# Two passes for the values of joint attention, a last projection split by tokens, and a residual spilled without its norm

## What is computed

```python
x = x + gmlp_mixer(rms_norm(x, a_norm_g), ...)
k, v = shared_kv(x, kv_norm_g, w_kv)
x = x + chunk_attention_mixer(rms_norm(x, b_norm_g), k, v, b_w_qz, b_rel_bias, b_w_out)  # 16 heads of 64
x = rms_norm(x, final_norm_g)            # end of the first block
h = rms_norm_2(x, norm_g)
y_a = hgrn2_branch(h ...)                # 8 heads of 128
y_b = mla_branch(h ...)                  # 8 heads of 128
merged = gates[0] * (y_a @ w_proj_a) + gates[1] * (y_b @ w_proj_b)
x = x + merged @ w_out                   # the last projection
return rms_norm_2(x, final_norm_g_2)
```

## Time and profile before

| | |
|---|---|
| median of three runs | 1359.68 us |
| profiled execution, its own time | 1360.59 us |
| its span, first to last instruction | 1358.8 us |
| mean granted TensorE clock | 0.992 |
| TensorE busy | 1306.7 us (96%) |
| VectorE, ScalarE, GpSimd busy | 719.0, 646.5, 493.8 us |
| DMA read, written | 124.97 MB, 10.49 MB |

### The profile page before, as it was taken

The page is one execution under the profiler, slowest core; times in us unless marked ns, Lnnn a source line. Parts: engine busy times, 40 slices in busy tenths (PEclk is TensorE's granted clock), DMA queues, the critical chain, the costliest instruction groups (busy, mean ns, idle before and its releaser), DMA issues.

```text
span 1358.8 us, 16181 instructions
## 1 busy us (share of the span) xinstructions
PE 1306.7 (96%) x6346; PEld 1084.1 (80%) x6346; DVE 719.0 (53%) x1256; ACT 646.5 (48%) x957; POOL 493.8 (36%) x206
## 2 busy tenths in 40 slices
PE   6999999999999999999998899999999999999985
PEld 4787888888888888888876788888887888888864
DVE  6464646552236465554766376766626546642325
ACT  4344444542334556464435466656546545542211
POOL 2454344434444323322334433333333333234430
PEclk9999999999999999999999999999999999999998
DMA  5542232334232322322224322222223222234421
GB/s 222 187 139 87 92 99 82 93 101 156 94 108 93 92 78 80 104 62 72 68 82 147 109 63 62 72 78 68 78 93 96 73 80 87 88 103 153 131 62 62
DMA packets 42155, 132.31 MB, mean 97 GB/s; under 512 B 6944, under 2 KB 9696, under 8 KB 41440
## 3 DMA queue, kind: packets, MB, share of 16 engines
q1 hardware_dynamic: 36704, 116.41, 27.2%
q10 hardware_dynamic: 5376, 14.87, 3.1%
HBM read 124.97 MB, written 10.49 MB: 100 GB/s over the span
## 4 chain that ended last, share of the span: by engine, by line
PE 78%; DVE 11%; ACT 6%; issue 2%; DMA 1%; POOL 1%; ACTq 0%; DVEq 0%; SPq 0%
PE banks L462 24%; PE banks L464 24%; PE banks L463 24%; DVE hd L1805 1%; PE banks L624 1%; PE banks L613 1%; DVE naccb L1705 1%; ACT L1232 1%; POOL wlo L452 1%; DVE hb L1802 1%; ACT L1233 1%; PE banks L856 1%; DVE acc L1478 1%; PE banks L735 1%; DMA x_kept<-x 1%
## 5 line engine op out<-in xcount | busy, mean ns | idle before, releaser
L452 POOL TENSOR_TENSOR wlo<-raw,whi 128x1024 fp32r<-128x1024 f32 (+2 forms) x202 | 493.6, 2446 | 829.8 <-ACT whi L973 829.8
L462 PE MATMUL banks<-hhi,whi 128*128 128x512 f32 x752 | 304.7, 405 | 4.5 <-POOL wlo L452 3.3
L973 ACT ACTIVATE whi<-raw 128x1024 fp32r<-128x1024 f32 (+2 forms) x202 | 210.2, 1041 | 201.8 <-PE banks L464 149.4
L464 PE MATMUL banks<-hlo,whi 128*128 128x512 f32 x752 | 294.3, 391 | 0.0
L463 PE MATMUL banks<-hhi,wlo 128*128 128x512 f32 x752 | 294.1, 391 | 0.0
L462 PE MATMUL banks<-yhi,whi 128*128 128x512 f32 x448 | 176.5, 394 | 0.0
L464 PE MATMUL banks<-ylo,whi 128*128 128x512 f32 x448 | 174.6, 390 | 0.0
L463 PE MATMUL banks<-yhi,wlo 128*128 128x512 f32 x448 | 174.4, 389 | 0.0
L462 PEld LDWEIGHTS banks<-hhi,whi 128*128 128x128 f32 x752 | 142.0, 189 | 33.2 <-issue 5.6
L464 PEld LDWEIGHTS banks<-hlo,whi 128*128 128x128 f32 x752 | 141.6, 188 | 30.6
L463 PEld LDWEIGHTS banks<-hhi,wlo 128*128 128x128 f32 x752 | 142.0, 189 | 26.8 <-issue 1.9
(11 more groups left out here) (359 smaller groups left out, 2116.1 us busy)
## 6 DMA issues: line engine op xcount, KB each, us to landing
raw<-w SPq DMA_DIRECT2D x194, 512.0 KB, 3.5
rel_tab<-relx ACTq DMA_DIRECT2D x1, 4096.0 KB, 21.4
tab<-rel_tab SPq DMA_DIRECT2D x16, 224.0 KB, 3.5
x<-xt SPq DMA_DIRECT2D x4, 512.0 KB, 6.5
x<-xt ACTq DMA_DIRECT2D x1, 2048.0 KB, 8.1
x_kept<-x ACTq DMA_DIRECT2D x1, 2048.0 KB, 7.3
parts_kept<-mcg SPq DMA_DIRECT2D x8, 256.0 KB, 4.4
mgt<-parts_kept SPq DMA_DIRECT2D x8, 256.0 KB, 3.9
```

The costliest lines, as they stand in the source:

```text
L452: nc.gpsimd.tensor_tensor(wlo[:, n % 4, 0:width], raw[:, n % 2, 0:width], f32(whi[:, n % 4, 0:width]), ALU.subtract).then_inc(lo_done, 1)
L462: nc.tensor.matmul(dst, a[0], b[0], start=first, stop=False)
L464: return nc.tensor.matmul(dst, a[0], b[1], start=False, stop=last)
L973: nc.scalar.activation(whi[:, n % 4, 0:width], raw[:, n % 2, 0:width], ACT.Copy).then_inc(hi_done, 1)
```

## The change

**Attention.** For each pair there are now two value tiles: in the one for head q, the 64 columns of side q hold the high half of that head's values and the other 64 the low half. A matmul with `phi` and one with `plo` then give the high terms in the rows of side q and the low terms in the other rows. ScalarE copies the low rows to `ao` (`lower_terms`), VectorE adds the two (`sum`), and the multiplication by `az` becomes a step of its own (`gated`), after this pair's maxima. Head 0 writes bank 0 instead of 2, head 1 bank 2 instead of 7 (at the last pair 7 and 2), so t=3 waits for head 1 only. `at_values` writes halves of 64 columns.

**Residual.** The spill is of `x` without the norm, issued on ScalarE's queue after the last slab `w2`. The diagonal, the wide matmul and the eight multiplications for it move to the loop of the `pb` slabs (`normed`).

**Last projection.** Tokens are done in two halves of 256, in the order `W3_ORDER` (g is the half, m the slab). The first three half slabs run k 0 to 6 first. Slabs 4 to 7 are kept in `yhi`, `ylo`, and their cuts wait for no buffer. The squares of the last tile are summed by TensorE itself; mean, reciprocal and root are on 128x2 (`factors`), and spread as at the border. Half 0 is normed and stored while half 1 is computed. `norm` is gone.

```diff
+W3B = (2, 3, 0, 1)
+W3_ORDER = [(0, 0), (0, 1), (1, 0), (0, 2), (0, 3), (1, 1), (0, 4), (0, 5), (1, 2), (0, 6), (0, 7),
+            (1, 3), (1, 4), (1, 5), (1, 6), (1, 7)]
+TOK_AT = 11
+OUT0 = [range(0), range(0, 3), range(3, 6), range(6, 8)]
+KEPT = AT["w3", KT // 2]
+HALF = [slice(S // 2 * g, S // 2 * (g + 1)) for g in range(2)]
...
+AO = [(0, 2)] * (PAIRS - 1) + [(7, 2)]
...
+        def av_at(q, half, t, side):
+            return av[q][:, 4 * half:4 * half + 4, t, BD * side:BD * (side + 1)]
...
+        def parts(n):
+            if n < KEPT:
+                return whi[:, n % 4, :], wlo[:, n % 4, :]
+            tiles = slice(2 * (n - KEPT), 2 * (n - KEPT) + 2)
+            return [u[:, tiles, :].rearrange("p k n -> p (k n)") for u in (yhi, ylo)]
...
-                        pe.wait_ge(auV.sem, auV.at("y0", i - 1))
+                        pe.wait_ge(auV.sem, auV.at("sum1", i - 1))
...
             def at_attended(i):
+                pe.wait_ge(auV.sem, auV.at("plo1", i))
                 for q in (1, 0):
-                    pe.wait_ge(auV.sem, auV.at("plo1", i))
                     for k in range(TT):
...
+                        for p in (phi, plo):
+                            last = nc.tensor.matmul(bank[AO[i][q]][:, k * P:S], av[q][:, i, k, :],
+                                                    p[:, q, AK[q][k]:AK[q][k] + KW[k]], start=k == 0 and p is phi,
+                                                    stop=k == TT - 1 and p is plo)
                     last.then_inc(auP.did(f"o{q}"), 1)
 
             at_values(0)
             for i in range(PAIRS):
+                if i >= 2:
+                    pe.wait_ge(auV.sem, auV.at("sum0", i - 2))
...
+            pe.wait_ge(auV.sem, auV.at("sum0", PAIRS - 2))
...
-                        for g in range(2):
-                            wide = nc.tensor.matmul(bank[3 - g], ones, diag[:, g, :], start=True, stop=True)
-                        wide.then_inc(n2P.did("wide"), 1)
+                        nc.tensor.matmul(bank[3], ones, diag[:, 0, :], start=True, stop=True).then_inc(n2P.did("wide"), 1)
...
+                if m == 1:
+                    pe.wait_ge(x3V.sem, x3V.at("diag"))
+                    nc.tensor.matmul(bank[5], ones, nfull[:, 1, :], start=True, stop=True).then_inc(x3P.did("wide"), 1)
...
-            pe.wait_ge(mgV.sem, mgV.all())
-            for m in range(KT):
-                if m >= 4:
-                    pe.wait_ge(w3V.sem, w3V.at(f"x{m - 4}"))
-                slab("w3", m, bank[m % 4], (mgh, mgl))
-            norm(n3, w3V.sem, w3V.all())
+            def out_slab(at, ks=range(KT)):
+                g, m = W3_ORDER[at]
+                n = AT["w3", m]
+                pe.wait_ge(lo_done, n + 1)
+                hi, lo = parts(n)
+                for k in ks:
+                    if at == 0:
+                        pe.wait_ge(mgV.sem, mgV.at("lo", k))
+                    cols = slice(k * P, (k + 1) * P)
+                    last = mm3(bank[W3B[at % 4]][:, HALF[0]], (hi[:, cols], lo[:, cols]),
+                               (mgh[:, k, HALF[g]], mgl[:, k, HALF[g]]), k == 0, k == KT - 1)
...
+            def out_tokens(g):
+                pe.wait_ge(w3V.sem, w3V.at(f"acc{g}{KT - 2}"))
+                pe.wait_ge(w3A.sem, w3A.at(f"sq{g}{KT - 1}"))
+                for b in range(2):
+                    blk = slice(S // 2 * g + P * b, S // 2 * g + P * (b + 1))
+                    to = bank[7][:, 2 * g + b:2 * g + b + 1]
+                    nc.tensor.matmul(to, nacc[:, blk], ones[:, 0:1], start=True, stop=False)
+                    tok = nc.tensor.matmul(to, nsq[:, (KT - 1) % 2, blk], ones[:, 0:1], start=False, stop=True)
+                tok.then_inc(w3P.did(f"tok{g}"), 1)
+
+            def out_wide(g):
+                pe.wait_ge(w3V.sem, w3V.at(f"diag{g}"))
+                nc.tensor.matmul(bank[6 - g][:, HALF[0]], ones, nr[:, 0, HALF[g]], start=True,
+                                 stop=True).then_inc(w3P.did(f"wide{g}"), 1)
+
+            pe.wait_ge(mgA.sem, mgA.all())
+            for at in range(2):
+                out_slab(at, done_keys)
+            pe.wait_ge(mgV.sem, mgV.at("b", KT - 2))
+            out_slab(2, done_keys)
+            for at in range(3):
+                out_slab(at, last_key)
+            for at in range(3, 2 * KT):
+                if at >= 4:
+                    g, m = W3_ORDER[at - 4]
+                    pe.wait_ge(w3V.sem, w3V.at(f"x{g}{m}"))
+                out_slab(at)
+                if at == TOK_AT:
+                    out_tokens(0)
+                if at == TOK_AT + 1:
+                    out_wide(0)
+            out_tokens(1)
+            out_wide(1)
...
-                if n >= 4:
+                if 4 <= n < KEPT:
                     act.wait_ge(slab_used, n - 3)
-                nc.scalar.activation(whi[:, n % 4, 0:width], raw[:, n % 2, 0:width], ACT.Copy).then_inc(hi_done, 1)
+                nc.scalar.activation(parts(n)[0][:, 0:width], raw[:, n % 2, 0:width], ACT.Copy).then_inc(hi_done, 1)
...
+                    got = bank[4 + t].rearrange("p (h v) -> p h v", v=P)
+                    for q in range(2):
+                        hi = nc.scalar.activation(av_at(q, half, t, q), got[:, :, BD * q:BD * (q + 1)], ACT.Copy,
+                                                  scale=rt1[:, 2, t:t + 1] if half == 0 else 1.0)
+                    hi.then_inc(avA.did(f"hi{t}"), 1)
...
+            def lower_terms(i):
+                for q in (1, 0):
+                    to, of = slice(BD * q, BD * (q + 1)), slice(BD * (1 - q), BD * (2 - q))
+                    act.wait_ge(auP.sem, auP.at(f"o{q}", i))
+                    if i >= 1:
+                        act.wait_ge(auV.sem, auV.at("sum0", i - 1))
+                    nc.scalar.activation(ao[to, :], bank[AO[i][q]][of, :], ACT.Copy).then_inc(auA.did(f"low{q}"), 1)
...
+            act.wait_ge(w2V.sem, w2V.at(f"x{KT - 1}"))
+            act.dma_start(xs, x[:, :, :]).then_inc(st_x, 16)
...
             act.wait_ge(n2V.sem, n2V.all())
-            act.dma_start(xs, x[:, :, :]).then_inc(st_x, 16)
...
+            def square(g, m):
+                act.wait_ge(w3V.sem, w3V.at(f"x{g}{m}"))
+                if m >= 2:
+                    act.wait_ge(w3V.sem, w3V.at(f"acc{g}{m - 2}"))
+                nc.scalar.activation(nsq[:, m % 2, HALF[g]], x[:, m, HALF[g]], ACT.Square).then_inc(w3A.did(f"sq{g}{m}"), 1)
...
                 for q in (1, 0):
                     rows = slice(BD * q, BD * (q + 1))
-                    dve.wait_ge(auP.sem, auP.at(f"o{q}", i))
-                    V.tensor_tensor(ay[rows, :], bank[(2, 7)[q]][rows, :], az[rows, :], ALU.mult).then_inc(auV.did(f"y{q}"), 1)
-                dve.wait_ge(auV.sem, auV.at("y0", i))
+                    dve.wait_ge(auA.sem, auA.at(f"low{q}", i))
+                    V.tensor_tensor(ay[rows, :], bank[AO[i][q]][rows, :], ao[rows, :], ALU.add).then_inc(auV.did(f"sum{q}"), 1)
+
+            def gated(i):
+                dve.wait_ge(asA.sem, asA.at("z", i))
+                dve.wait_ge(auV.sem, auV.at("sum0", i))
+                V.tensor_tensor(ay[:, :], ay[:, :], az[:, :], ALU.mult).then_inc(auV.did("y"), 1)
+                dve.wait_ge(auV.sem, auV.at("y", i))
...
-                dve.wait_ge(asA.sem, asA.at("z", i - 1))
                 outputs(i - 1)
+                maxima(i)
+                gated(i - 1)
                 probabilities(i)
...
-            for k in range(KT):
-                V.scalar_tensor_tensor(x[:, k, :], x[:, k, :], cols("fin1", KT)[k], bank[2], ALU.mult,
-                                       ALU.mult).then_inc(n2V.did(f"x{k}"), 1)
...
+            dve.wait_ge(mtP.sem, mtP.all())
+            V.tensor_tensor(nfull[:, 1, :].rearrange("p (t n) -> p t n", n=P), ident.unsqueeze(1).to_broadcast([P, TT, P]),
+                            rt2[:, 7, :].unsqueeze(2).to_broadcast([P, TT, P]), ALU.mult).then_inc(x3V.did("diag"), 1)
+
+            def normed(k):
+                V.scalar_tensor_tensor(x[:, k, :], x[:, k, :], cols("fin1", KT)[k], bank[5], ALU.mult,
+                                       ALU.mult).then_inc(x3V.did(f"x{k}"), 1)
 
             for m in range(KT):
+                if m == 3:
+                    dve.wait_ge(ld_x3, 16)
+                    dve.wait_ge(x3P.sem, x3P.at("wide"))
+                if 3 <= m < 7:
+                    normed(2 * m - 6)
+                    normed(2 * m - 5)
...
+            def residual(g, m):
+                if g == 0:
+                    dve.wait_ge(w3P.sem, w3P.at(f"m{m}"))
+                else:
+                    used("w3", m)
+                V.tensor_tensor(x[:, m, HALF[g]], x[:, m, HALF[g]], bank[W3B[W3_ORDER.index((g, m)) % 4]][:, HALF[0]],
+                                ALU.add).then_inc(w3V.did(f"x{g}{m}"), 1)
...
+            def factors(g):
+                two = slice(2 * g, 2 * g + 2)
+                dve.wait_ge(w3P.sem, w3P.at(f"tok{g}"))
```

(60 more changed lines are left out.)

126 lines of the change are left out of this document (46 added, 80 removed).

## The result

The changed kernel takes 1341.4 us in the median (1340.5 to 1344.2), before 1360.5 beside it: ratio 0.9862 [0.9847, 0.9876]. So the change is worth 19.1 us, not the 26.7 forecast, and 1341.4 lies just outside the range of 1327 to 1341. The profiled execution took 1344.19, span 1342.2: the slowest of the four.

The account below looks back on a forecast made before the run. TensorE, 96% busy, was taken as the bound: only fewer matmuls, less waiting or less lower clock help. Terms -8.3 - 7.6 - 10.8 = -26.7 took 1359.7 to 1333.0 us, range 1327 to 1341.

Parts of the forecast that it names:

- Part 1: Attention's values: two matmul passes per head instead of three; -9.6 + 0.4 + 0.9 = -8.3 us.
- room ahead of `sum1`: Attention pairs: `sum1` ends 0.7 us before score group t=3 is due, so its wait was priced at nothing.
- Part 2: Start of HGRN heads, residual spilled without norm: waits -5.9 and lower clock -1.7, together -7.6 us.
- Part 3, start and width: Last projection: `mgl` wait and lower clock gone -6.4, 256-column matmuls +1.2, sums inside the stream +1.3 us.
- `lo7`: Start of last projection: needed at 1298.7, may be held until 1297.4, so covered by 1.3 us.
- The step that failed: Last projection: bank and cut waits have 2.8 us per half slab against 1.3 us on VectorE.
- Its own signs of being wrong: Last-stage pitch over 0.13, ScalarE copies over 0.7 us after their head's matmuls, or first HGRN cuts awaiting raw data.
- Part 3, end: After VectorE's last add: 9.2 us to the end instead of 16.1, -6.9 us, from -8 to -5.5.
- Rival (c): Last projection: the tail or `lo7` gives less, that part's gain at half, 1338 us; chance 0.10.

Follow-up runs that it names:

- e9: Changed kernel with ScalarE's cut of slab 6 moved behind the first square and slab 7's behind the third, same kernel as e4; 1335.3 us, ratio 0.9821.
- e12: Changed kernel with only ScalarE's cut of slab 7 moved from ahead of the last projection's first square to behind it; 1337.9 us, ratio 0.9832.
- e3: Kernel before the change with only the last projection done in two halves; 1357.4 us, ratio 0.9972.
- e6: Changed kernel with only VectorE's order altered, sums of squares two half slabs behind the adds; 1336.4 us, ratio 0.9828.
- e7: Changed kernel with both orders altered, squares ahead of cuts on ScalarE and adds ahead of sums on VectorE; 1337.6 us, ratio 0.9835.
- e4: Changed kernel with ScalarE's cut of slab 6 moved behind the first square and slab 7's behind the third; 1333.5 us, ratio 0.9808.
- e10: Kernel of e9 with ScalarE's first low copy of each attention pair cut into 16 pieces of 32 columns; 1337.7 us, ratio 0.9842.

## Why the prediction missed

From the traces, stage by stage, by the same landmarks in each (first statistics; maxima of the first pair; start of the token sums at the border; first and last matmul of the projection; end), us:

| stage | before | after | e9 |
|---|---|---|---|
| to the first statistics | 111.3 | 114.2 | 113.35 |
| to the first pair's maxima | 341.7 | 342.5 | 342.5 |
| attention pairs, to the token sums | 239.2 | 230.35 | 230.3 |
| to the projection (before: to its wait) | 599.1 | 591.5 | 589.4 |
| projection, wait included | 51.0 | 52.9 | 47.15 |
| last matmul to the end | 16.55 | 10.8 | 10.9 |

- **Part 1** (-8.3): right. 0.8 lost in the value slabs, 8.8 won in the pairs, -8.0 in all. The turn fell by 1.23 us to 23.42 as the doubled head saving of 1.2 said, with 0.8 us of room ahead of `sum1` where 0.7 was worked out.
- **Part 2** (-7.6): right. -7.6 in this trace, -9.7 in e9's, -7.4 timed alone. The traces of before and after have a granted clock of 0.83 and 0.86 from 690 to 700, e9's has 1.00 there, and that and 0.6 us less of waiting for `ddiag` are the difference between the two. Both `wlo` waits went with the lower clock, and neither the spill nor the nine operations in the merge brought a new one.
- **Part 3, start and width** (-6.4 + 1.2 + 1.3 = -3.9): right for a kernel without the new wait. e9 has -3.9 (51.0 to 47.15), pitch 0.120. `lo7` wasn't missed: TensorE passes it without a wait although GpSimd held `mgl` up, 2.77 us instead of 0.69, from 1282.78 to 1285.55 beside its subtraction of 1282.56 to 1285.00. The Trainium skill, "SBUF — State Buffer", Who interferes with whom, says that a VectorE instruction with two SBUF inputs contends with a GpSimd instruction that reads SBUF. The trace agrees, and as worked out the cover shrinks (to 0.5 us, as TensorE wants `lo7` at 1286.1) and no time is lost.
- **The step that failed** is the sentence "The other waits (banks, cuts) have 2.8 us per half slab against 1.3 us on VectorE". It compares rates, where the start of the stage is a question of order. ScalarE's queue held four cuts ahead of the first square, and their times are set by transfers (3.4 to 3.6 us) and GpSimd (2.5 us), not by TensorE. For attention's copies the prediction did name what is queued behind them; here it should have walked the queue in the same way: the last merge slab ends at 1278.5; cut 1.1, GpSimd 2.6, transfer 3.6, cut 1.1 and so on to 1294, then square 0.4, sum 2.2 and add 0.4 to 1297, against a bank wanted at 1293. The 1.3 us that it gave VectorE for a half slab also leaves out that the sum beside a GpSimd subtraction takes 2.2. The price is 4.0 for the wait + 1.7 for the lower clock behind it (7 us at 0.76) = 5.7 us. And the warning stood in the trace of before, where cuts also stand ahead of the squares (there they wait for TensorE's use of a slab, not for a transfer). The first square came at 1321.33, VectorE idled 17.81 us, and its sum took 2.21 (timeline of ScalarE, its last waiting cut and the square; then of VectorE):

```profile
1320.36 1.06 ACT L973 ACTIVATE whi<-raw 128x1024 fp32r<-128x1024 f32 x1 [4.56 <-PE banks L464]
1321.33 0.62 ACT L1413 ACTIVATE nsq<-x 128x512 f32<-128x512 f32 x1
```

```profile
1303.48 0.69 DVE L2001 TENSOR_TENSOR x<-x,banks 128x512 f32<-128x512 f32 x1 [6.97 <-PE banks L464]
1321.98 2.21 DVE L1453 COPY nacc<-nsq 128x512 f32<-128x512 f32 x1 [17.81 <-ACT nsq L1413]
1324.11 0.68 DVE L2001 TENSOR_TENSOR x<-x,banks 128x512 f32<-128x512 f32 x1
```

  The add of slab 1 ends at 1324.8, and slab 5 wants its bank at 1325.8 (72 matmuls of 0.234 ahead of the last end, 1342.65). That it cost nothing there is owed to 1.0 us of cover: four whole slabs of 5.6 us fill four banks, and halves fill them in half the time. An idle of 17.8 us on an engine that releases banks should have been read as the next bottleneck, and the prediction read only TensorE's waits at this place. Its own signs of being wrong don't touch this queue either: the pitch stayed at 0.120, ScalarE's copies started within 0.7 us of their head's matmuls, and a cut at the start of the HGRN heads did wait 0.85 us for raw data (at 715.44), without a wait on TensorE.
- **Part 3, end** (-6.9, 16.1 to 9.2): the mechanism is right, the size is off. From the last add it took 10.5 us:

```profile
1331.72 0.42 DVE L2067 TENSOR_TENSOR x<-x,banks 128x256 f32<-128x256 f32 x1 [0.35 <-PE banks L487]
...
1334.91 1.22 PE L1003 MATMUL banks<-nr,cst 128*128 128x256 f32 x2 [1.15 <-DVE nr L2086]
...
1336.17 3.22 DVE L2090 SCALAR_TENSOR_TENSOR x<-x,vec,banks 128x256 f32<-128x256 f32 x8 [1.32 <-PE banks L1003]
```

  The wide matmul took 1.22 us instead of 0.75, at a granted clock of 0.50; in e12, at 1.00, it took 0.70. Of the nine traces with this tail four have the short one (e3, e6, e7, e12) and five the long one, so 0.5 of the 1.3 comes and goes. The eight scalings are the 3.2 foreseen, but from their end (1339.4) to the end of the span it is 2.8 us, not 2.3. The rest, 0.3, is in the small steps; no run takes these two apart. +1.3 in all.
- **Not from the change**: the profiled execution took 2.9 us more in its first stage than the one of before. The same program reached that landmark at 113.35 in its second trace, and e12, which doesn't differ from it up to there, at 111.03 (last section).

The sum, corrected with what the traces show: -26.7 + 5.7 + 1.3 = -19.7; the medians say -19.1 and -19.2. Rival (c), part 3 at half, had the right place and named tail and `lo7` as its reasons; only the tail was one of them. Without the queued squares (e4, e9) the forecast of 1333.0 stands beside 1333.5 and 1335.3, although the tail's 1.3 is lost there as well; that they lie so close is in part luck.

## What to carry to other kernels

When tiles are made smaller, the same number of buffers covers less time: price again every queue that stood under the old cover, even one that was free before. At the start of a stage walk the in-order queues, instruction by instruction, and don't compare mean rates; an operation that waits for memory and stands ahead of one that frees a buffer ties the buffer to the transfer. The remedy is either order, the freeing operation ahead of the waiting one on one engine or of its consumer on the other; doing both gained nothing here.

## What the runs showed of the hardware

The same first stage runs at different clocks in different executions. In it TensorE waits 3.0 us for `wlo` in each kernel (in the trace of before up to 44.95, in that of after up to 44.97), and the clock behind that wait differs; the table's rows from 42 to 50 us are, for the kernel before, the changed kernel and e12:

```profile
42.00:50.00 8.00, 5.05 (x22) 4.16 (x23) 0.69 (x2) 2.60 (x4) 5.33 (x3) 1.00 0.43 117
```

```profile
42.00:50.00 8.00, 5.03 (x12) 3.97 (x13) 0.71 (x2) 2.55 (x4) 5.22 (x3) 0.64 0.41 118
```

```profile
42.00:50.00 8.00, 5.30 (x23) 4.42 (x24) 0.44 (x1) 2.71 (x3) 5.67 (x3) 1.00 0.44 131
```

TensorE is busy 5 us of 8 in each, with 22, 12 and 23 matmuls. The first statistics then start at 111.3, 114.2 and 111.0. Of the 14 traces three have a mean of 1.00 in these 8 us (statistics at 111.0 to 111.3), nine 0.79 (112.4 to 113.4) and two 0.64 or 0.65 (114.2 and 114.3), and e9 and e12, which don't differ before the last merge, are 2.3 us apart. So up to 3 us of a single span of this kernel says nothing of a change. A span is better compared from a landmark behind that stage: from the first statistics to the end it is 1228.0 in the changed kernel's first trace and 1226.9 in its second.

VectorE's fp32 copy of 128x256 (`nacc<-nsq`) took 2.2 to 2.3 us each time that it ran beside a GpSimd subtraction, and 0.28 to 0.30 otherwise (e6: 1291.74 to 1294.03 beside 1291.48 to 1293.88). That it is GpSimd that holds it is read from these times; no run takes the subtraction away.

Fifteen more copies of 64x32 from PSUM on ScalarE in e10 cost 0.85 us, 0.06 each, less than half of what the pitch of larger ones had suggested to me.
